# Hybrid decoder layer on one core: the 32 experts staggered by one, their weights in one ring of ten places, and a rewritten router tail

## The reference

```
mixed = g[:, :, 0] * y_conv + g[:, :, 1] * y_mla
h = h + mixed @ w_out[l]
h = h + moe(rms_norm(h, ffn_norm_w[l]), router_w[l], ...)

logits = (xt @ router_w + router_b); top_val, top_idx = lax.top_k(logits, 4)
gates = jax.nn.softmax(top_val, axis=-1)
# per expert e, for the tokens xb that chose it, with their gates wb
g, u = split(xb @ w_gate_up[e] + b_gate_up[e])          # 1024 x 2048
act = (min(g, 7) * sigmoid(1.702 * min(g, 7))) * (clip(u, -7, 7) + 1)
y  += scatter((act @ w_down[e] + b_down[e]) * wb)       # 1024 x 1024
```

## Time and profile before

| | us |
|---|---|
| median of 3 runs | 1149.29 (1147.57 to 1149.74) |
| profiled execution, its own time | 1151.61 |
| its span, first to last instruction | 1149.7 |
| PE busy | 1063.8 (93% of the span) |
| DVE busy, ACT busy | 250.0, 170.3 |
| moved by DMA | 431.90 MB, mean 376 GB/s |

### The profile page before, as it was taken

The page is one execution under the profiler, slowest core; times in us unless marked ns, Lnnn a source line. Parts: engine busy times, 40 slices in busy tenths (PEclk is TensorE's granted clock), DMA queues, the critical chain, the costliest instruction groups (busy, mean ns, idle before and its releaser), DMA issues.

```text
span 1149.7 us, 15140 instructions
## 1 busy us (share of the span) xinstructions
PE 1063.8 (93%) x6271; PEld 476.3 (41%) x6271; DVE 250.0 (22%) x656; ACT 170.3 (15%) x341; POOL 6.8 (1%) x17
## 2 busy tenths in 40 slices
PE   7999989799999999999999999999999999999996
PEld 5788876533333333333333333333333333333332
DVE  1588742721111111111111111111111111111101
ACT  3453340411100000000000000000000000000000
POOL 1000000000000000000000000000000000000000
PEclk9999999899999999999999999999999999999998
DMA  9843275599999999999999999999999999999995
GB/s 289 301 126 112 74 291 222 182 428 416 427 429 429 428 429 428 428 428 429 428 428 429 429 429 429 427 429 428 382 422 429 429 429 428 429 429 429 428 428 219
DMA packets 52643, 431.90 MB, mean 376 GB/s; under 512 B 5075, under 2 KB 23838, under 8 KB 28174
## 3 DMA queue, kind: packets, MB, share of 16 engines
q1 hardware_dynamic: 51984, 431.04, 90.7%
q0 software_dynamic: 272, 0.43, 0.2%
q10 hardware_dynamic: 366, 0.15, 0.1%
HBM read 430.55 MB, written 1.05 MB: 375 GB/s over the span
## 4 chain that ended last, share of the span: by engine, by line
PE 56%; DMA 39%; ACT 2%; DVE 1%; issue 1%; SPq 1%; ACTq 0%; DVEq 0%
DMA arena<-in_w_down 29%; PE psum L781 17%; PE psum L804 14%; DMA arena<-in_w_gate_up 10%; PE psum L589 5%; PE psum L504 4%; PE psum L814 3%; PE psum L642 2%; PE psum L680 2%; PE psum L751 2%; PE psum L766 1%; ACT arena L1044 1%; PE psum L792 1%; PE psum L759 1%; PE psum L580 0%
## 5 line engine op out<-in xcount | busy, mean ns | idle before, releaser
L781 PE MATMUL psum<-arena 128*64 128x512 f32 x2048 | 448.7, 594 | 9.5 <-DMA arena<-in_w_gate_up 9.0
L804 PE MATMUL psum<-arena 128*64 128x512 f32 x1024 | 233.1, 604 | 51.3 <-DMA arena<-in_w_down 37.1
L781 PEld LDWEIGHTS psum<-arena 128*64 128x64 f32 x2048 | 144.2, 137 | 311.6 <-issue 292.3
L1345 DVE TENSOR_SCALAR arena<-psum 128x512 f32<-128x512 f32 x32 | 22.1, 691 | 760.7 <-PE psum L781 749.9
L804 PEld LDWEIGHTS psum<-arena 128*64 128x64 f32 x1024 | 71.4, 138 | 190.9 <-issue 137.2
L1032 ACT COPY arena<-psum 128x512 f32<-128x512 f32 x32 | 18.7, 585 | 490.8 <-PE psum L751 490.8
L814 PE MATMUL psum<-arena 64*128 64x512 f32 x256 | 63.7, 615 | 0.7 <-ACT arena L1048 0.7
L751 PEld LDWEIGHTS psum<-arena 128*128 128x128 bf16 x1536 | 48.4, 98 | 29.2 <-issue 29.2
L589 PE MATMUL psum<-arena 128*128 128x256 f32 x256 | 58.8, 381 | 0.3 <-ACT arena L963 0.3
L1048 ACT COPY arena<-psum 128x512 f32<-128x512 f32 x32 | 18.7, 585 | 265.9 <-PE psum L804 265.9
L751 PE MATMUL psum<-arena 128*128 128x64 bf16 x1536 | 52.2, 194 | 4.0 <-DVE arena L1278 4.0
(11 more groups left out here) (218 smaller groups left out, 497.0 us busy)
## 6 DMA issues: line engine op xcount, KB each, us to landing
arena<-in_w_gate_up SPq DMA_DIRECT2D x128, 2048.0 KB, 26.2
arena<-in_w_down SPq DMA_DIRECT2D x63, 2048.0 KB, 21.9
arena<-in_w_in SPq DMA_DIRECT2D x9, 1024.0 KB, 6.1
arena<-in_w_in SPq DMA_DIRECT2D x8, 512.0 KB, 9.0
arena<-in_w_out SPq DMA_DIRECT2D x1, 4096.0 KB, 17.2
arena<-in_w_o_mla SPq DMA_DIRECT2D x1, 2048.0 KB, 10.0
arena<-in_conv_pw_w SPq DMA_DIRECT2D x1, 2048.0 KB, 15.9
arena<-in_w_down SPq DMA_DIRECT2D x4, 512.0 KB, 21.0
```

What stands on the lines that cost most here:

```text
L781: last = mm(b[64 * half:64 * half + 64, :], xe[i][:, k, :], gu[i][c][:, j, o + half * 512:o + half * 512 + 512], start=(k == 0 and bias_la ...
L804: last = mm(Y[64 * c:64 * c + 64, :], aT[:, j, 64 * h:64 * h + 64], dn[h][:, j, c * 512:(c + 1) * 512], start=(h == 0 and j == 0), stop=(h ...
L1345: ts(g_s, G, LIMIT, None, ALU.min).then_inc(S.g_ready, 1)
```

## The change

One edit of the whole program, in these parts:

1. **Order of the experts on PE.** gate_up(n) is followed by down(n-1), then gather(n+1), scatter(n-1), turn(n+1), turn_act(n). The result of the last expert is copied on ACT (`result_out`) once DVE has used the sigmoid's tile, since both now share memory. The rows of the next expert are copied on DVE (`rows_out`) and no more on ACT. The loop body holds five experts and not two, with three sets of the small tiles (`SIDE`).
2. **One ring.** All ten areas hold any piece. Piece k goes to place k mod 10 and waits until piece k-10 has been used; the order is that of the use: gate and up of experts 0 and 1, down of 0, gate and up of 2, down of 1, and so on.
3. **First pieces.** The areas are laid out anew so that `w_out` (now two halves by columns) is loaded right behind the attention, and pieces 0 to 9 only wait for the dense part's tiles (4 for the attention mixer, 5 to 7 for the convolution mixer, 8 and 9 for `w_out`'s halves).
4. **Router tail.** `project_out` runs in five parts (row tile 0: two halves; row tile 1: one half, two quarters), each added to x on DVE. Turning, router products and ranks stand between the parts. The norm's weight is applied behind the gather. Expert 0 is gathered in float32 straight from `h1` (`gather_first`, 16 products), and the split into bf16 parts (now eight smaller pieces) comes behind it. `residual` moves into gate_up(0).
5. **Dense part.** Eight products on zeros stand at the start (`busy`), the small turned parameters come behind the first projections, a `gate_tile` is cut in two so that half of it lies between scores and their use in every step, DVE does nine convolution steps earlier, and `channel_sum` on DVE leaves one product each for `lnmu` and `lnvar`.

```
 EXTRA = SEQ * TOPK // SLOTS
 GC, GR = 4, 2
 DC, DR = 2, 4
+PER, RING10 = GC + DC, 10
+ROUND = 5
+SIDE = [0, 1, 0, 1, 2]
...
+def gate_up_piece(n, c):
+    return PER * n - 2 + c if n else c
+def down_piece(n, h):
+    return PER * n + 8 + h if n < E - 1 else PER * E - 2 + h
...
-        gu = [[grid((A0, B0)[i] + 4096 * c, GR, 2 * FF) for c in range(GC)] for i in range(2)]
-        dn = [grid(D0 + 4096 * h, DR, D) for h in range(DC)]
+        CHUNK = 4096
+        slot_at = [A0 + CHUNK, A0 + 2 * CHUNK, A0, A0 + 3 * CHUNK, D0, D0 + CHUNK] + [B0 + CHUNK * c for c in range(4)]
+        slot_gu = [grid(at, GR, 2 * FF) for at in slot_at]
+        slot_dn = [grid(at, DR, D) for at in slot_at]
...
+            def load_piece(k):
+                load(*piece_number(k), k % RING10)
...
             sp.wait_ge(*piece_used["g", 3])
-            load_gu(0, 0, 1)
+            load_piece(0)
             sp.wait_ge(*piece_used["g", 5])
-            load_gu(0, 0, 2)
+            load_piece(1)
             sp.wait_ge(S.oT_ready, 4)
+            for c in range(2):
+                sp.dma_start(wout[c], a["w_out"][0][:, c * 512:(c + 1) * 512].rearrange("(k p) c -> p k c", p=P)
+                             ).then_inc(in_wout, 16)
             for t in range(2):
-                sp.dma_start(xres[t], x[t * P:(t + 1) * P, :]).then_inc(in_res, 16)
-            sp.dma_start(wout, a["w_out"][0].rearrange("(k p) c -> p k c", p=P)).then_inc(in_wout, 16)
-            sp.dma_start(fnw, a["ffn_norm_w"][0].partition_broadcast(P)
-                         ).then_inc(in_router, 16)
+                sp.dma_start(h1[:, t, :], x[t * P:(t + 1) * P, :]).then_inc(in_res, 16)
             sp.dma_start(rwt, a["router_w"][0].rearrange("(k p) e -> p k e", p=P)).then_inc(in_router, 16)
...
-            for c in (0, 3):
-                load_gu(0, 0, c)
+            for k in (2, 3):
+                load_piece(k)
+            sp.wait_ge(S.ymix_ready, 4)
+            load_piece(4)
             sp.wait_ge(S.mix_ready, 4)
-            for h in range(DC):
-                load_dn(0, h)
...
-            EARLY = 20
-            with sp.Fori(0, EARLY // 2) as it:
-                for u in range(2):
-                    next_gu(2 * it + (2 + u), u)
-                    next_dn(2 * it + (1 + u))
-            next_dn(EARLY + 1)
-            with sp.Fori(0, (E - EARLY - 4) // 2) as it:
-                for u in range(2):
-                    next_gu(2 * it + (EARLY + 2 + u), u)
-                    next_dn(2 * it + (EARLY + 2 + u))
-            next_gu(E - 2, 0)
-            next_dn(E - 2)
-            next_gu(E - 1, 1)
-            sp.wait_ge(S.dn_done, DC * (E - 2) + 1)
-            load_dn(E - 1, 0)
-            sp.wait_ge(S.dn_done, DC * (E - 1))
+            for k in (5, 6, 7):
+                load_piece(k)
+            for k in (8, 9):
+                sp.wait_ge(S.h1_ready, 3 if k == 8 else 5)
+                load_piece(k)
+            with sp.Fori(0, (E - 2) // ROUND) as it:
+                for k in range(RING10, RING10 + ROUND * PER):
+                    e, piece = piece_number(k)
+                    sp.wait_ge(S.used, ROUND * PER * it + (k - RING10 + 1))
+                    load(ROUND * it + e, piece, k % RING10)
+            sp.wait_ge(S.used, PER * E - 2 - RING10 + 1)
+            load_piece(PER * E - 2)
+            sp.wait_ge(S.used, PER * E - 1 - RING10 + 1)
...
+            nc.gpsimd.memset(idle, 0.0).then_inc(S.cols_clear, 1)
...
+            def busy(bank, times, n):
+                for _ in range(times):
+                    mm(psum[:, bank, 0:n], idle[:, 0:P], idle[:, 0:n], start=True, stop=True)
+            pe.wait_ge(S.cols_clear, 3)
+            busy(6, 3, SEQ)
             pe.wait_ge(in_ident, 16)
             pe.wait_ge(in_attn, 16)
             filled("pa", nc.tensor.transpose(fill("pa")[:, 0:KD], rows[R_ATTN:R_ATTN + KD, 0, :], ident[0:KD, 0:KD]))
+            busy(6, 5, SEQ)
...
-                between = s % 4 == 0 and s > 0
+                gate_tile(s, 4, KD)
+                if s % 4 == 0 and s:
+                    values(s // 4 - 1)
                 if s + 1 < 2 * H:
-                    gate_tile(s + 1, 0, 4 if between else KD)
-                if between:
-                    values(s // 4 - 1)
-                    gate_tile(s + 1, 4, KD)
...
+            pe.wait_ge(S.lnsum_ready, 1)
+            filled("lnmu", mm(fill("lnmu")[:, 0:SEQ], ones, lnsum[:, 0, :], start=True, stop=True))
...
+            project_out(OUT_PARTS[0], 0, KD)
+            project_out(OUT_PARTS[1], 0, KD)
+            project_out(OUT_PARTS[2], 0, 2)
+            turn_state(OUT_PARTS[0])
+            project_out(OUT_PARTS[2], 2, 5)
+            turn_state(OUT_PARTS[1])
+            project_out(OUT_PARTS[2], 5, KD)
+            pe.wait_ge(S.hT_ready, 2)
+            router(0, 0, KD)
+            project_out(OUT_PARTS[3], 0, 4)
+            turn_state(OUT_PARTS[2])
+            project_out(OUT_PARTS[3], 4, KD)
+            project_out(OUT_PARTS[4], 0, 2)
+            pe.wait_ge(S.mask_ready, 1)
+            fill(("rank", 0))
+            mm(small_bank[:, RANK:RANK + E], tri, maskt[:, 0, :], start=False, stop=True, skip_group_check=True)
+            filled(("rank", 0), mm(small_bank[:, RANK + E:RANK + 2 * E], ones, maskt[:, 0, :], start=False, stop=False,
+                                   skip_group_check=True))
+            project_out(OUT_PARTS[4], 2, 4)
+            turn_state(OUT_PARTS[3])
+            pe.wait_ge(S.hT_ready, 3)
+            router(1, 0, 4)
...
+            def gather_first(t):
+                pe.wait_ge(S.place_ready, t + 1)
                 for k in range(KD):
...
+                    if bias_last:
+                        pe.wait_ge(*((S.xe_half, 1) if c == 0 else (S.xe_ready, 1)))
+                    if bias_last and c == GC - 1:
+                        for t in range(2):
+                            for part in range(2):
+                                residual(t, part)
...
-            def item(n, i, gu_loads, dn_loads, final=False):
-                gate_up(n, i, gu_loads)
-                if not final:
-                    gather(n + 1, 1 - i)
-                scatter(n - 1, 1 - i)
-                if not final:
-                    turn(n + 1, 1 - i)
-                turn_act(n)
-                down(n, (dn_loads, dn_loads), in_pieces=final)
...
+            gate_up(0, SIDE[-1], gu_of(0), bias_last=True)
+            b = fill("cnt")[:, 0:E]
+            mm(b, ones, maskt[:, 0, :], start=True, stop=False)
+            filled("cnt", mm(b, ones, maskt[:, 1, :], start=False, stop=True))
+            turn(0, SIDE[-1])
             pe.wait_ge(S.gate_ready, 2)
             b = fill("gt")
             for t in range(2):
                 last = nc.tensor.transpose(b[0:E, t * P:(t + 1) * P], gate[:, t, :], ident)
             filled("gt", last)
-            for bank in (4, 5, 7):
-                free(bank)
-            pe.wait_ge(in_bias, 48)
-            gate_up(0, 0, 16, bias_last=True)
-            turn(0, 0)
             down_biases()
+            gather(1, SIDE[0])
+            turn(1, SIDE[0])
             turn_act(0)
-            down(0, (16, 16))
-            gather(1, 1)
-            turn(1, 1)
-            with pe.Fori(0, E // 2 - 1) as it:
-                item(2 * it + 1, 1, 16 * it + 16, 32 * it + 32)
-                item(2 * it + 2, 0, 16 * it + 32, 32 * it + 48)
-            item(E - 1, 1, 16 * (E // 2), 16 * E, final=True)
-            scatter(E - 1, 1)
+            with pe.Fori(0, (E - 2) // ROUND) as it:
+                more = 16 * (ROUND * PER // RING10) * it
+                for u in range(ROUND):
+                    n, after = ROUND * it + (1 + u), SIDE[(u + 1) % ROUND]
+                    gate_up(n, SIDE[u], gu_of(1 + u, more))
+                    down(n - 1, dn_of(u, more))
+                    gather(n + 1, after)
+                    scatter(n - 1, SIDE[u - 1])
+                    turn(n + 1, after)
+                    turn_act(n)
+            gate_up(E - 1, SIDE[0], gu_of(E - 1))
+            down(E - 2, dn_of(E - 2))
+            scatter(E - 2, SIDE[-1])
+            turn_act(E - 1)
+            down(E - 1, dn_of(E - 1), in_pieces=True)
+            scatter(E - 1, SIDE[0])
...
-            def result_out(n):
-                act.wait_ge(S.dn_done, DC * n + DC)
+            def result_out(n, last_act=None):
+                if last_act is not None:
+                    act.wait_ge(S.act_ready, last_act + 1)
                 nc.scalar.copy(y_s, Y).then_inc(S.y_ready, 1)
...
-            conv_taps(len(taps))
+                conv_taps(7 if s in (4, 8, 12) else 4)
+            def channel_sum(y):
+                link(tt(lnsum, y[:, 0:2, :], y[:, 2:4, :], ALU.add))
+                tt(lnsum[:, 0, :], lnsum[:, 0, :], lnsum[:, 1, :], ALU.add).then_inc(S.lnsum_ready, 1)
+            dve.wait_ge(S.conv_step, CT * TAPS)
...
+            def out_part(i):
+                t, c, n = OUT_PARTS[i]
```

(11 more changed lines are left out.)

628 lines of the change are left out of this document (347 added, 281 removed).

## The result

The changed kernel takes 1155.09 us (median of 11 runs, 1152.64 to 1158.45). The kernel before, run beside it, takes 1151.28 us (11 runs). The ratio is 1.0047 with a 95% interval of 1.0035 to 1.0059: about 0.5% **slower**, where I forecast 1136 us. The profiled execution took 1157.40 us, with a span of 1155.6, against 1136.8 in the forecast's sum: 18.8 us are missing.

The account below looks back on a forecast made before the run. Weight transfers (4.89 us a piece), not PE, were taken as the bound: flow from 251.9 us, 178 pieces and 1.2 of dips gave 1124.1, plus 12.7 made 1136.8, 12.9 under the profiled span; forecast 1136 us, range 1130 to 1142.

Parts of the forecast that it names:

- (a) to (d): Start, attention, mixers and router tail: gate_up(0) starts at 215.9 us, 13.7 earlier.
- (e): First experts: transfers pause some 9 us until piece 4 is used, flow from 251.9; 178 pieces and dips end at 1124.1.
- (f): End of the experts: 12.7 us from last byte to end, against 16.5 before; sum 1136.8.
- the gap: Transfers near 250 us: some 9 us without flow, since piece 14 needs piece 4 used, at 249.9.
- the 32.3: PE's work, with small pauses, ahead of using piece 4: 32.3 us, including gate_up(0) 13.9 and down_biases 3.6.
- less gain: Rival: (a) and attention bring nothing and Silu is late, or waits and low clock cost 5 us; 1142 to 1147, chance 0.16.
- (a): Start of the dense part: work on zeros lifts TensorE's clock, gain 2.3 us, bounds 0 and 3.
- 178 x 4.893: Experts behind the gap: 178 pieces left from 251.9 us at 4.893 us each, ending at 1122.9.
- the transfers still break: Rival: each turn of the new loop costs the old seam's 3.2 us, five turns 16 us; 1152, no gain, chance 0.04.
- a rate under 425 GB/s: Sign of being wrong, in the experts' transfers, where 428 GB/s was forecast.
- more gain: Rival: PE's products from gate_up(0) to piece 4's use take 27.9 us without pauses; 1130 or less, chance 0.14.
- PE becomes the bound: Rival: in the experts, over 1.7 us of new waits per pass on PE makes the kernel slower, chance 0.06.

Follow-up runs that it names:

- e4: Changed kernel without the four b_down products (that part of the output left out), waits kept: 1138.49 us, ratio 0.991.
- e10: Changed kernel with the b_down products moved from ahead of the second expert to behind the loop of experts, nothing left out: 1139.09 us, ratio 0.9921.
- e1: Kernel before with TensorE's loop written over six experts (5 turns) instead of two (15 turns), nothing else changed: 1157.09 us, ratio 1.0061.
- e2: Changed kernel with all loops over two experts instead of five and the ten places fixed by kind: 1157.47 us.
- e11: Changed kernel with a ring of nine places instead of ten and loops over three experts instead of five: 1152.47 us.
- e14: As e10, with TensorE's two transposes in turn made eight times each, 28 more instructions an expert: 1152.71 us.
- e9: Kernel before with 8640 tiny memsets in a straight line on idle GpSimd, TensorE's code and loop unchanged: 1190.55 us, 3.5% slower.
- e16: e10 run once more, unchanged: 1140.26 us.
- e6: Changed kernel with the b_down products made over 128 rows, 96 of them zero, instead of 32: 1150.47 us.
- e7: As e2, with down(0) made ahead of the second expert's gate and up, and b_down moved behind them: 1157.25 us.
- e12: As e10, with the first expert's down ahead of the second's gate and up in transfers, places and work: 1144.70 us.

## Why the prediction was wrong

**(a) to (d)** held: gate_up(0) started 0.3 us off the sum, of which the cancelling of 1.3 and 1.6 us within it is luck.

**(e), the step that decides,** failed in both of its terms, and (f) only passed it on.

*Its first term, the gap.* "It is used at 215.9 + 1.7 + 32.3 = 249.9": the 32.3 had every product at its duration at the upper clock, b_down 3.6, gather 1.5, though I had added 1.7 for a cold clock earlier, and though rows 4 show 0.50 and 0.91 in just such stretches. It measured 258.1, and the gap 16.0 us for 9. e4, without these products, and e10, with them behind the loop, have no fall of the clock there, and piece 14 lands 13.3 and 11.1 us earlier. A smaller slip stands beside it: by the sum the first pieces last until about 243 us, but the use of piece 3 stands behind `residual`, and piece 13 landed at 246.5. The rival "less gain" named this cause ("the low clock around the gap cost 5 more"), too small and too seldom. The Trainium skill ("TensorE: Matmul & The Clock Gate", "Part 1: The HAM clock gate") says that the array's clock is throttled by default and activity releases it; the kernel before agrees, with 0.50 over 223 to 227 us, where PE is busy 1.15 of 4 us. The 0.52 over 239 to 256 us is less plain, since PE is busy 16.22 of these 17 us; what stood ahead of the fall were short products with waits of 0.79 and 0.45 us. I used that rule for (a), where it gave a gain, and did not ask here whether the new order would lose the clock.

*Its second term, 178 x 4.893.* The 4.893 us a piece were read from rows 2 and 3, from loops over two experts, and carried over to loops over five. They measured 4.949, and the rate in GB/s doesn't show it: 427 against 428. The cause is shown from three sides: the old order with a long body has it (e1), the new order with short ones hasn't (e2, e11), and a few more instructions bring it back (e14); e9 shows that fetches alone suffice, without TensorE's stand of 4.6 us at each turn. The sum had no term for the instructions' own fetches, that is, it put them at nothing. My last rival, "the transfers still break", came nearest, since it put a loss down to the new loop, but nothing breaks at its turns: the first share of each piece still lands every 4.894 us, and the lag grows all along. I put it at 0.04 with rows of the *old* loop as the evidence. My sign of being wrong, a rate under 425 GB/s, could not have shown the lag either. The Trainium skill has what was missing ("Runtime: NRT & Kernel Launch", "Instruction fetch mechanics"): TensorE's instruction memory holds 128 KiB and is refilled in blocks of 16 KiB by a DMA queue of its own, at a cost "mostly hidden". The trace has 1691 TensorE instructions between two turns of a loop over five experts, 1019 over three and 2013 over six; at 64 bytes each, which is that section's 256 to a block of 16 KiB, that makes 108, 65 and 129 KB by estimate. The runs agree with the size only roughly: bodies of two and three experts are never fetched again, but those of six always are, though 129 KB is still under 128 KiB (131 KB), and five is on the edge (18, 25, 27, 54 and 63 packets for about the same length of body, and 64 for 117 KB). The change's nine packets a turn are 147 KB, more than its whole body of 108. They don't agree with "mostly hidden": here a fetch costs more than its own time, since the DMA engine that carries it falls behind for good while the queue never runs dry.

*What e10 adds.* With the clock up and the fetches gone, the sum's order of events holds to the end: piece 14 lands at 255.7 (by the sum 256.8), piece 189 at 1113.5 (1114.3), and the span is 1136.3 against 1136.8, or 1138.4 in e16. The structure was right and two terms of one step were mis-sized, by 10.0 and 9.8 us, together more than the 13 us that the change brings. (In the rival "more gain" the 27.9 us of products are 2 us short: by the terms of (e) they sum to 29.9.) "PE becomes the bound" did not come true: a pass of the changed kernel takes 26.0 us.

**What stays open.** Why five experts stay resident in e10 (no fetch between 352 and 1094 us) and not in the changed kernel: b_down's instructions no longer stand ahead of the loop and shift it by a small part of a block, but I didn't vary the position alone. What brings the clock down near 240 us: 32 rows aren't needed for it (e6), nor are the products themselves (e7, e12), and the same program has a fall at the end in one execution (e16) and none in another (e10). And whether the ring of nine with late b_down, in the order of the change, would be faster still: that was not run.

## What to carry to other kernels

A loop body is bought in instruction memory: before a loop is written over more items to make a ring's indices come out, look at the packets of the instruction queue, and weigh a ring whose period is short against one place more of lead (here the ring of nine with three experts gave back 9.8 us of lag and cost 3.9 of lead, e11). A transfer rate at full share does not say that the pieces land in time; where sixteen engines share each piece, the slowest one's landings are what counts, and as long as the queue never drained, a lag was never made good here. And price the short steps ahead of a release at the lower clock.

## What I had not expected of the hardware

- By the landings, GpSimd's instruction fetches (8 KB) all fell on one DMA engine, TensorE's (16 KB) went round eight of sixteen. 67 of the former, 0.55 MB in an execution that moves 432 MB, made it 40 us longer.
- A packet of instructions delays its engine by about twice what its record lasts (0.6 for 0.31 us) or nearly half as much again (1.5 for 1.08 us).
- The seam at 830 us of the kernel before, 3.2 us in which the transfers thin out, brings the engines together again (spread 6.9 to 0.8 us in e1, 19 to 0.6 in e9). The forecast counted its removal as gain alone.
